# A hybrid decoder trunk on one core: the shifted bias rows are spread in DRAM in two transfers instead of one

## What is computed

```
rel = t[:, None] - keys[None, :]
bias = transpose(table[t5_bucket(rel)], (2, 0, 1))     # one column of the table per B, C, D head
s = where(rel >= 0, s + bias, NEG_INF)
# C: top-k keys by sum over 8 index heads of relu(q_idx . k_idx) * w_idx, then softmax over those
```

## Time and profile before

| | us |
|---|---|
| median of three runs | 725.83 (724.16 to 727.79) |
| the profiled execution | 724.13 |
| its span, first to last instruction | 722.3 |
| PE busy | 678.1 (94%) |
| DVE busy | 431.6 (60%) |
| ACT busy | 330.0 (46%) |
| POOL busy | 241.6 (33%) |
| TensorE clock granted, mean | 0.972 of full |

### The profile page before, as it was taken

The page is one execution under the profiler, slowest core; times in us unless marked ns, Lnnn a source line. Parts: engine busy times, 40 slices in busy tenths (PEclk is TensorE's granted clock), DMA queues, the critical chain, the costliest instruction groups (busy, mean ns, idle before and its releaser), DMA issues. The chain is left out here.

```text
span 722.3 us, 10492 instructions
## 1 busy us (share of the span) xinstructions
PE 678.1 (94%) x3840; PEld 546.9 (76%) x3840; DVE 431.6 (60%) x1068; ACT 330.0 (46%) x751; POOL 241.6 (33%) x209
## 2 busy tenths in 40 slices
PE   6997999999999998789999999999999999988996
PEld 4885977888897765468998897788889876445896
DVE  4311697889888665641271169787978975556114
ACT  5422634656343547751343355356533363666121
POOL 1532351253245632000625443325323663200030
PEclk9998999999999989989999999999999997999999
DMA  8467964423223110303362687442322221030202
GB/s 247 130 220 233 268 197 116 132 73 111 67 73 106 42 58 1 118 0 118 90 200 63 178 273 225 140 146 73 104 74 73 73 74 59 0 117 1 88 25 94
DMA packets 66644, 80.96 MB, mean 112 GB/s; under 512 B 10737, under 2 KB 52337, under 8 KB 66593
## 3 DMA queue, kind: packets, MB, share of 16 engines
q1 hardware_dynamic: 66593, 80.29, 36.1%
HBM read 69.76 MB, written 13.93 MB: 116 GB/s over the span
## 5 line engine op out<-in xcount | busy, mean ns | idle before, releaser
L642 POOL TENSOR_TENSOR w_low<-w_raw,w_high 128x512 fp32r<-128x512 f32 (+2 forms) x156 | 198.7, 1305 | 390.4 <-ACT w_high L682 390.4
L1174 PE MATMUL bank<-uT,w_high 128*128 128x512 f32 x400 | 160.9, 402 | 0.0
L1176 PE MATMUL bank<-uT,w_low 128*128 128x512 f32 x400 | 159.2, 398 | 0.0
L1175 PE MATMUL bank<-uT,w_high 128*128 128x512 f32 x400 | 159.0, 398 | 0.0
L790 ACT ACTIVATE probs<-probs,negmax 128x128 f32<-128x128 f32 (+3 forms) x160 | 89.0, 557 | 91.4 <-DVE negmax L1029 91.1
L1174 PEld LDWEIGHTS bank<-uT,w_high 128*128 128x128 f32 x400 | 76.2, 190 | 18.4 <-issue 1.0
L1176 PEld LDWEIGHTS bank<-uT,w_low 128*128 128x128 f32 x400 | 76.0, 190 | 18.0
L1175 PEld LDWEIGHTS bank<-uT,w_high 128*128 128x128 f32 x400 | 76.1, 190 | 16.4
L682 ACT ACTIVATE w_high<-w_raw 128x2048 fp32r<-128x2048 f32 (+2 forms) x39 | 72.7, 1864 | 26.5 <-DMA w_raw<-in_w_out 23.3
L1174 PE MATMUL bank<-w_high,mix 128*128 128x256 f32 x256 | 72.5, 283 | 1.0 <-DVE mix L1114 1.0
L1176 PE MATMUL bank<-w_high,mix 128*128 128x256 f32 x256 | 71.6, 280 | 0.0
(11 more groups left out here) (150 smaller groups left out, 1089.8 us busy)
## 6 DMA issues: line engine op xcount, KB each, us to landing
w_raw<-in_w_in SPq DMA_DIRECT2D x27, 1024.0 KB, 5.4
w_raw<-in_w_out SPq DMA_DIRECT2D x8, 1024.0 KB, 4.9
parts_dram<-staging SPq DMA_DIRECT2D x12, 512.0 KB, 4.9
strips<-strips_dram SPq DMA_DIRECT2D x24, 256.0 KB, 4.2
dqk<-parts_dram SPq DMA_DIRECT2D x24, 256.0 KB, 4.3
hX<-in_x SPq DMA_DIRECT2D x8, 512.0 KB, 6.0
strips_dram<-table_dram SPq DMA_DIRECT2D x1, 3328.0 KB
qidx<-parts_dram SPq DMA_DIRECT2D x12, 256.0 KB, 4.2
```

The source lines that it names most:

```text
L642: ins = nc.gpsimd.tensor_tensor(w_low[:, s, ks, 0:w], w_raw[:, s, ks, 0:w], w_high[:, s, ks, 0:w].bitcast(F32), ALU.subtract)
L1174: nc.tensor.matmul(out_ap, lh, rh, start=start, stop=False)
L1175: nc.tensor.matmul(out_ap, lh, rl, start=False, stop=False)
L1176: return nc.tensor.matmul(out_ap, ll, rh, start=False, stop=stop)
```

## The change

The spreading becomes a helper, `spread_rows(a, b)`, that spreads rows a to b. At `unit cq 1` of layer 0 only D's rows and the mask (8 to 12, 1.31 MB) are spread, and SP no longer waits there for them. The wait and the load of the mask move to the step `unit qi 1`, ahead of the loads of `qidx`. The rows of B and C (0 to 7, 2.10 MB) are spread at the step `scores 0 0 2`, with no wait behind them. `strips_stored` then counts to 32, and SP waits for that at `norm 0`, ahead of the first load of one of B's strips.

```diff
@@ -538,6 +538,12 @@
             load_group(2)
             STRIP_ROW = {"B": 0, "C": 4, "D": 8}
 
+            def spread_rows(a, b):
+
+                shifts = bass.AP(tensor=table_dram.tensor, offset=table_dram.offset + a * TABLE_W + P - 1,
+                                 ap=[[TABLE_W, b - a], [-1, P], [1, SEQ]])
+                sp.dma_start(strips_dram[a:b], shifts).then_inc(strips_stored, 16)
+
             def load_strip(dst, row):
                 return sp.dma_start(dst, strips_dram[row])
 
@@ -547,11 +553,13 @@
                     sp.wait_ge(table_copied, 1)
                     sp.dma_start(table_dram, table[:]).then_inc(table_stored, 16)
                     sp.wait_ge(table_stored, 16)
-                    shifts = bass.AP(tensor=table_dram.tensor, offset=table_dram.offset + P - 1,
-                                     ap=[[TABLE_W, 13], [-1, P], [1, SEQ]])
-                    sp.dma_start(strips_dram, shifts).then_inc(strips_stored, 16)
+                    spread_rows(STRIP_ROW["D"], 13)
+                if (l, step) == (0, ("unit", "qi", 1)):
+
                     sp.wait_ge(strips_stored, 16)
                     load_strip(mask[:], 12).then_inc(mask_loaded, 16)
+                if (l, step) == (0, ("scores", 0, 0, 2)):
+                    spread_rows(0, STRIP_ROW["D"])
                 if step in STACK_AT:
@@ -589,6 +597,8 @@
                     j = step[1]
                     h = JOBS[j][1]
                     sp.wait_ge(shifted, jobs_scored(l, j))
+                    if l == 0 and j == 0:
+                        sp.wait_ge(strips_stored, 32)
                     load_strip(strips[:, h, :], STRIP_ROW[BRANCHES[j // HEADS + 1]] + h
                                ).then_inc(strips_loaded[h], 16)
```

## The result

| | before | changed | ratio, 95% interval |
|---|---|---|---|
| with the first profiles, median of 4 runs each | 726.81 us | 718.95 us | 0.9883 (0.9842 to 0.9924) |
| the changed kernel again, later, 6 runs against 23 | 727.15 us | 716.74 us | 0.9863 (0.9821 to 0.9905) |
| the profiled executions | 724.13 us | 717.92 us | |
| their spans | 722.3 us | 716.1 us | |
| TensorE clock granted, mean | 0.972 | 0.976 | |

The forecast was 717.5 us in a range of 713.5 to 721.5; the first median is 718.95. Medians are over all executions, while the ratios compare fast executions only and leave out slow ones (one of the 23, and two of ten in the experiment with the weights behind the store).

A forecast was written before the change was run, and what follows sets the result against it. PE, busy for 94% of the span, was taken as the bound. Taking 7.95 us from the profiled 724.13 gave 716.2, or 717.9 from the median of the runs; the forecast was 717.5, range 713.5 to 721.5.

The forecast's parts named there:

- The stall and its price: At `idx 0` of layer 0: 5.07 us of PE idle and 2.88 us of low clock, together 7.95 us, would go.
- everything downstream would keep the gain: From `dq 0` to `gb 0` both layers run at the same pace, so the whole 7.95 us carries to the end.
- Five rows: 1.31 MB, 4.4 us: First spreading: 4.4 us of moving at 296 GB/s and 3.9 around, landing near 43.9, at worst 51.0.
- 3.9 us around it: Part of a spreading's time taken not to shrink with size: issue, start and landing, 3.9 us beside the moving.
- The store's 2.68 us: Store of `qi 0`, issued at 49.5, would take layer 1's 2.68 us instead of 6.84, so SP goes on at 52.2.
- the 1.4 us to spare at `idx 0`: `qidx` would be ready at 57.8 and PE done with `dq 0` at 59.2, so the stall is gone.
- The second spreading: Eight rows issued at 101.0 land at 112.0, at most 116.4; `bq` weights at about 116, at worst 122.4; nothing lost.
- The slack of 3 to 4.5 us: Time between `bq` weights being there at about 116 and ACT taking them up at 119.0 or 120.5.
- the prediction's last sentence: The prediction is wrong if PE still waits for `qidx`, or a new wait for weights follows the second spreading.
- theory A: From the experiments: a transfer keeps as many DMA engines busy as rows, about 11 us regardless; later transfers wait on them.
- Rival 1: Low clock between `gb 0` and `gb 1` of layer 0 goes too: 1.58 us more gained, 716.3 us; chance 0.30.

## Why the prediction was right, and which of its steps were not

**The stall and its price: right.** The whole gain was to be the wait at `idx 0` and the low clock behind it, priced at 7.95 us by laying layer 0 beside layer 1. On ACT it was 14.15 - 6.36 = 7.79 us, in the medians 7.86. The experiment that kept PE busy confirms the two parts; that medians and term agree to 0.1 us is luck. That everything downstream would keep the gain was right as well.

**"Five rows: 1.31 MB, 4.4 us": wrong.** The term that failed is the first spreading's duration, 8.3 us from issue to landing. It measured 13.43 where SP waits for it, and the share of busy engines in the same window of before, 0.81 of them and not 1, was the hint I read over. The "3.9 us around it" was misread as well: to about 50.6 two engines were still moving rows, so some 2 us of the 3.9 were moving. The Trainium skill (DMA: Bandwidth & Descriptors, "Why a DMA increments its semaphore by 16 and not by 1") states it: a DMA issued from SP runs on the largest number of engines up to 16 that divides the slowest dimension of both sides, and on the lowest-numbered ones. The traces agree: 0.20, 0.31, 0.53 and 0.81 of the engines for 3, 5, 8 and 13 rows, and a second transfer that waits for the first (which engines these are, the traces don't show). The forecast survived because the landing was covered by the store in either case, as its upper bound had said (51.0): in the profile the mask's load went out at 50.30, right behind the issue of the store.

**The store's 2.68 us, and the 1.4 us to spare at `idx 0`: too good.** It was 4.05 us: the packets have five engines bringing weights of `dv` to 52.3, and the store waits for the last engine. The margin at `idx 0` is nothing: 0.03 us of idle in the first profile, 0.3 us of waiting in two of the experiments that share this part of the code.

**The second spreading: right that it costs nothing, wrong by how much.** Landing 14.28 us after its issue instead of 11.0 (upper bound 15.4), and the weights of `bq` there at 120.0 instead of 116. SP waited for 8.4 us at `norm 0`, but before it had waited there for 10.2 us, for DVE; from the pace of before (122.53 - 118.23 = 4.30 us behind `gb 0`) it was held about 2 us longer than DVE alone would have. The slack of 3 to 4.5 us was used up: ACT waited 0.21 us for the weights in the first profile and not at all in the second. By the letter of the prediction's last sentence that 0.21 us is a sign of being wrong; PE had no wait from it. Another wait of ACT, 1.28 us for weights at 81.14, the prediction had not seen either; it cost PE nothing. By theory A this is one more term by bytes that should have gone by rows.

**Rival 1, the second low-clock stretch: not decided.** Layer 0 won its 1.58 us in the profile (119.20 - 111.03 = 8.17), and layer 1 lost it again:

```profile
457.71 0.60 ACT L774 ACTIVATE gate<-bank 128x512 f32<-128x512 f32 x1 [0.41 <-PE bank L1186]
467.47 0.60 ACT L774 ACTIVATE gate<-bank 128x512 f32<-128x512 f32 x1 [3.77 <-PE bank L1186]
```

9.76 us here, 8.17 before: the two cancel. The profiled span fell by 6.2 us and not by 7.95, and the read-outs show where: this execution was 0.43 us late at `dq 0` already, and of the 127.98 - 119.20 = 8.78 us that it was ahead at `gb 1` of layer 0 it had 465.71 - 457.71 = 8.00 left at `gb 0` of layer 1. Low-clock stretches elsewhere fell otherwise and account for about 0.3 of those 0.8 us; the rest is not traced. With the matmuls of the two profiles laid side by side, the lead falls from 8.54 to 5.56 us between 253 and 266 of the changed kernel, whose granted clock is 0.50 from 255 to 265, and comes back to 8.25 us at 316 of the kernel before, whose granted clock is 0.50 from 310 to 315.

Ten of twenty such waits were followed by the low clock, five in each layer. The Trainium skill's account (TensorE: Matmul & The Clock Gate, Part 1) of a monitor that runs freely, which the prediction weighed against the rival, fits that. But the rival spoke of layer 0, and there the low clock came again in 4 of the 5 profiles where the stall at `idx 0` had already brought it, and in 1 of the 5 where it had not. That leans towards the rival, and five profiles on each side are too few to tell.

**What stays open.** Whether the spreading could use all 16 engines, and what that would give: no run tried it. Whether the earlier stall makes the later low clock more likely.

## What to carry to other kernels

Price a DMA by its outermost dimension before its bytes: read the DMA share in its window, multiply by 16, and see who in the queue needs those same engines. Where an engine waits for a chain of small transfers, ask which large one stands anywhere in that chain; here, moving it one place back only handed the wait to the next link. Where two layers run the same list, the undisturbed one is a good forecast of the other.

## What I had not expected of the hardware

- Transfers of 3, 5, 8 and 13 rows of the same shape kept 0.20, 0.31, 0.53 and 0.83 of the DMA engines busy, at 75, 110, 205 and 294 GB/s, and splitting five rows into three and two made them land 10 us later (23.25 us against 13.43).
- SP's own issue of a transfer can stretch: 3.89 us for the weights of `bq` behind the eight rows, 7.55 and 5.14 us behind the two small transfers, against 0.4 us usually. Transfers of few rows are not the only cause, nor always one: in the kernel before, two weight loads at 127.98 took 7.19 us to issue with no spreading under way, and behind the five rows at 43.00 the issue took 0.38 us. What decides it stays open. A DMA issue is not always free for the issuer.
- Some 5 us of useless matmuls made the kernel faster (0.9952, 0.9914 to 0.9990; 1.86 us at that place), by keeping the clock at 2.4 GHz.
